# Where the last scaling of the output rows is done in an encoder step: VectorE alone, or VectorE and GpSimd

## What is computed

```python
def rmsnorm(x, g):
    xf = x.astype(jnp.float32)
    r = lax.rsqrt(jnp.mean(xf * xf, axis=-1, keepdims=True) + EPS)
    return (xf * r).astype(x.dtype) * g

def hier_moe(x, ...):
    ...                                  # top-1 group, top-2 experts of 16
    return x + out.reshape(bsz, L, D_MODEL)

y_prompt = rmsnorm(xp, norm_final)
y_sample = rmsnorm(xs, norm_final)
```

## Time and profile before

| | |
|---|---|
| median of three runs | 1203.53 us (1202.56 to 1205.54) |
| the profiled execution's own time | 1205.74 us |
| its span | 1204.0 us |
| TensorE busy, share of the span | 1144.2 us, 95% |
| VectorE busy | 715.8 us, 59% |
| ScalarE busy | 564.6 us, 47% |
| GpSimd busy | 120.6 us, 10% |
| mean granted TensorE clock | 0.983 of full speed |

### The profile page before, as it was taken

How to read it: one execution, slowest core, us unless ns; L and a number is a source line. 1 busy time by engine, 2 the same in 40 slices (tenths; PEclk the granted TensorE clock), 3 DMA queues, 4 the chain that set the end, 5 groups by cost and what they waited for, 6 DMA issues and landing times.

```text
span 1204.0 us, 18490 instructions
## 1 busy us (share of the span) xinstructions
PE 1144.2 (95%) x7908; PEld 1035.7 (86%) x7908; DVE 715.8 (59%) x850; ACT 564.6 (47%) x709; POOL 120.6 (10%) x147
## 2 busy tenths in 40 slices
PE   4999999999999999999899999999899999999994
PEld 4998779999987899999899999989757878788873
DVE  4424574775368743332434743534679998888884
ACT  4424473334386731221313632311166868778763
POOL 2002341000134100000000000000001000000051
PEclk9999998999999999999999999999899999999998
DMA  9231110222310222332435612201799999999995
GB/s 292 85 131 36 36 40 1 89 88 72 79 45 2 71 71 79 97 85 74 149 100 195 214 53 71 71 1 36 274 356 379 421 416 381 387 402 390 368 267 151
DMA packets 95038, 197.27 MB, mean 164 GB/s; under 512 B 4208, under 2 KB 71960, under 8 KB 82664
## 3 DMA queue, kind: packets, MB, share of 16 engines
q1 hardware_dynamic: 87328, 169.88, 40.2%
q0 software_dynamic: 5440, 18.76, 5.4%
q10 hardware_dynamic: 2184, 7.39, 1.5%
HBM read 178.41 MB, written 17.61 MB: 163 GB/s over the span
## 4 chain that ended last, share of the span: by engine, by line
PE 73%; DVE 10%; ACT 8%; issue 4%; DMA 4%; ACTq 0%; SPq 0%; POOL 0%; DVEq 0%; POOLq 0%
PE ps L2241 46%; PE ps L1032 6%; DVE buf_r L966 4%; ACT buf_r L959 3%; PE ps L1042 3%; PE ps L2646 2%; PE ps L2662 1%; DMA buf<-in_w_gate_e 1%; PE ps L2344 1%; PE ps L2373 1%; DMA buf<-in_w_in 1%; DVE buf_r L1181 1%; ACT buf_r L461 1%; PE ps L2374 1%; PE ps L2386 1%
## 5 line engine op out<-in xcount | busy, mean ns | idle before, releaser
L2241 PE MATMUL ps<-buf_r,buf_r 128*128 128x288 f32 (+1 forms) x4560 | 603.0, 293 | 12.8 <-DVE buf_r L465 6.5
L2241 PEld LDWEIGHTS ps<-buf_r,buf_r 128*128 128x128 f32 x4560 | 590.9, 190 | 17.3 <-issue 9.2
L966 DVE TENSOR_TENSOR buf_r<-buf,buf_r 128x2048 fp32r<-128x2048 f32 x92 | 205.1, 2284 | 0.0
L1032 PE MATMUL ps<-buf_r,buf_r 128*128 128x512 f32 x720 | 174.6, 398 | 0.0
L959 ACT CAST buf_r<-buf 128x2048 fp32r<-128x2048 f32 x92 | 170.9, 1908 | 0.1
L446 DVE TENSOR_TENSOR buf_r<-buf,buf_r 128x2048 fp32r<-128x2048 f32 (+2 forms) x49 | 107.5, 2196 | 103.8 <-ACT buf_r L440 103.7
L1032 PEld LDWEIGHTS ps<-buf_r,buf_r 128*128 128x128 f32 x720 | 133.4, 188 | 29.5 <-issue 0.5
L440 ACT CAST buf_r<-buf 128x2048 fp32r<-128x2048 f32 (+2 forms) x53 | 96.6, 1824 | 109.1 <-PE ps L2241 55.1
L1042 PE MATMUL ps<-buf_r,buf_r 128*128 128x512 f32 x384 | 89.8, 390 | 0.5 <-DVE buf_r L1209 0.5
L1042 PEld LDWEIGHTS ps<-buf_r,buf_r 128*128 128x128 f32 x384 | 72.0, 188 | 15.8 <-DVE buf_r L1209 0.9
L461 ACT CAST buf_r<-ps 128x512 fp32r<-128x512 f32 (+2 forms) x41 | 30.0, 731 | 75.9 <-PE ps L1016 63.2
(11 more groups left out here) (331 smaller groups left out, 1269.8 us busy)
## 6 DMA issues: line engine op xcount, KB each, us to landing
buf<-in_w_gate_e SPq DMA_DIRECT2D x32, 1024.0 KB, 8.3
buf<-in_w_up_e SPq DMA_DIRECT2D x32, 1024.0 KB, 7.9
buf<-in_w_down_e SPq DMA_DIRECT2D x32, 1024.0 KB, 7.4
buf<-in_w_in SPq DMA_DIRECT2D x16, 1024.0 KB, 5.5
buf<-in_w_in SPq DMA_DIRECT2D x17, 512.0 KB, 4.9
buf<-in_w_mem_kv SPq DMA_DIRECT2D x8, 1024.0 KB, 5.9
y_rows<-buf ACTq DMA_DIRECT2D x14, 512.0 KB, 8.0
buf<-in_x_prompt SPq DMA_DIRECT2D x8, 512.0 KB, 5.6
```

The source lines that it names most:

```text
L966: nc.vector.tensor_tensor(e_lo(t), e_raw(t), e_hi(t), ALU.subtract).then_inc(wl_ready, 1)
L1032: last = nc.tensor.matmul(bank(b), r32(a[:, k, :]), w[:, i, :], start=(k == 0 and j == 0), stop=(k == KD - 1 and j == 2))
L2241: last = nc.tensor.matmul(out, a, b, start=(k == 0 and j == 0), stop=(k == len(parts) - 1 and j == 2))
```

## The change

The order of the tail on VectorE becomes: add 0, add 1, finish 0, add 2, add 3, finish 2, add 4, finish 4. Chunks 1 and 3 are finished by GpSimd, each in two instructions: X times the row factor, a wait for the completion of that, then X times the gains. A new semaphore, fin_pool, counts these four. SyncE waits on it for chunks 1 and 3 and on fin_ready for the others, still in the order of the chunks.

```diff
@@ moe_sp
             for m, (t0, n) in enumerate(CH):
-                sp.wait_ge(fin_ready, m + 1)
+                if m % 2:
+                    sp.wait_ge(fin_pool, m + 1)
+                else:
+                    sp.wait_ge(fin_ready, m // 2 + 1)
                 dst = O["y_prompt"][0, t0:t0 + n, :] if m < 4 else O["y_sample"][0]
                 out_dma(sp, dst, X[:n, m, :], hn_stored)
@@ moe_pool
                 add_rows(pool, y_rows, R12O, 32)
+            pool.wait_ge(gains_loaded, 32)
+            for j, m in enumerate((1, 3)):
+                t0, n = CH[m]
+                pool.wait_ge(x3_ready, m + 1)
+                pool.wait_ge(ri_ready, N_F + m + 1)
+                pool.tensor_scalar(X[:n, m, :], X[:n, m, :], RI[:n, 17 + m:18 + m], None, ALU.mult).then_inc(fin_pool, 1)
+                pool.wait_ge(fin_pool, 2 * j + 1)
+                pool.tensor_tensor(X[:n, m, :], X[:n, m, :], NF[:n, :], ALU.mult).then_inc(fin_pool, 1)
@@ moe_dve
                 nc.vector.tensor_tensor(X[:n, m, :], X[:n, m, :], bank(SC_BANK[m], 2)[:n], ALU.add).then_inc(x3_ready, 1)
-                if m:
+                if m in (1, 3):
                     finish(m - 1)
             finish(NC_ - 1)
```

More of the change, by code:

```diff
@@ L521, in encoder_step @@
         fin_loaded = [sem(f"fin_loaded{i}") for i in range(2)]
-        sc_psum, x3_ready, fin_ready = (sem(n) for n in ("sc_psum", "x3_ready", "fin_ready"))
+        sc_psum, x3_ready, fin_ready, fin_pool = (sem(n) for n in ("sc_psum", "x3_ready", "fin_ready", "fin_pool"))
         yol_ready = sem("yol_ready")
```

## The result

| | before | after |
|---|---|---|
| median | 1203.53 us, 5 runs | 1209.36 us, 5 runs |
| lowest to highest | 1202.56 to 1205.54 | 1207.12 to 1211.62 |
| ratio of the runs | | 1.0043, 95% interval 1.0026 to 1.0059 |
| profiled execution | 1205.74 us, span 1204.0 | 1211.62 us, span 1209.9 |

What follows compares the result with a forecast made beforehand. VectorE bounds the tail for 7 us, then a latency chain; 0.45 us on the late last addition and 0.36 on the last finish give +0.81 us, so 1204.3 us from the 1203.53 median; range 1202.2 to 1207.2.

Steps and rivals of the forecast that it cites:

- What bounds the kernel: Tail: VectorE bound for 7 us, then a latency chain; removing two finishes gains 0.46 us, not 2.4.
- the price of the first step: GpSimd's multiplication of X by the row factor, chunks 1 and 3: taken as 1.05 us, lower bound 0.95.
- the upper bound: Most that GpSimd's multiplication by the row factor was taken to cost: 2.39 us, the two-input product's time.
- The rule of the Trainium skill: GpSimd runs one-input operations at roughly line rate; two-input ones take about twice as long as on VectorE, speaking against the change.
- The shut-out: VectorE's finishes and GpSimd's instructions exclude each other; a held finish ends 1.08 us behind GpSimd; additions from PSUM are free.
- the sum: Tail timeline with shut-out: last addition 0.45 us late, last finish 0.36 more, end +0.81 us; chance 0.65.
- d: Length of GpSimd's multiplication by the row factor, taken as 1.05 us; last finish ends at 1199.30 + 2d.
- The 0.12 us that a held instruction saves: GpSimd's instruction for chunk 3, held by finish 2, has 0.12 us of its start already behind it.
- Rival 1: Slow row-factor multiplication on GpSimd: +3.3 us at d = 2.3, +3.8 at 2.39 (1207.3); chance 0.08.
- its formula: Slow row-factor multiplication, finish 2 going first: last output issue at 1202.04 + d against 1200.62.
- The end of the span: Span ends 3.4 us after the last output DMA is issued.
- Rival 2: GpSimd's first multiplication starts late, its first d 5.0: +4.8 us, 1208.3; near +7 by the skill's figure; chance 0.03.

Runs made afterwards that it cites:

- a_second_alone: Kernel after without GpSimd's first step (row factor left out for chunks 1 and 3, time only): 1204.19 us, ratio 0.9996 to the kernel before.
- a_broadcast: Kernel after with GpSimd's first step written as a product with the row factor broadcast along the row: 1206.01 us, ratio 1.0013 to the kernel before.
- c_only3: Kernel after with only chunk 3 finished by GpSimd, chunk 1 back on VectorE: 1208.56 us, ratio 1.0030 to the kernel before.
- b_scalar: Kernel before plus four GpSimd multiplications by a row factor on scratch, beside VectorE's finishes: one execution, 1205.50 us.
- c_only1: Kernel after with only chunk 1 finished by GpSimd, chunk 3 by VectorE: 1205.12 us, ratio 1.0008 to the kernel before.

## Why the prediction was wrong

**What bounds the kernel**: right. The tail is a chain of latency behind a VectorE that is busy for 7 us, and taking two finishes out of it is worth 0.46 us; a_second_alone measured 0.45. That it came out so closely is in part luck: the same gain of addition 4 was 0.06 us in the first trace of the kernel after and 0.40 in the second, by when TensorE let addition 3 in.

**The step that failed is the price of the first step.** "I take 1.05, since it reads one tile as the cast does." It takes 2.83 to 2.86 us. I had put the upper bound at 2.39, as if a scalar could not cost more than a second tile. It does. The value lies above the upper bound, so the range was wrong from that line on. The numbers of the earlier trace rows are right, but they are those of casts and clearings; the trace of before has no row of GpSimd's arithmetic with a scalar, and I let the number of inputs stand for the form.

The prediction also said that "every one-input row is at 1 ns per column". That was not so. The groups of instructions of the kernel before have a selection, also with one input, beside a clearing of the same shape:

```profile
L1500 POOL TENSOR_SCALAR_AFFINE_SELECT buf<-buf 128x128 f32<-128x128 f32 x4 | 1.0, 282 | 0.1
...
L1494 POOL MEMSET buf<- 128x128 f32 x3 | 0.5, 204 | 0.0
```

The selection takes 282 ns for 128 columns, 2.2 ns per column, and the clearing 204. Read against the clearing of 1024 columns (952 ns), some 100 ns of it do not go with the width; taking the same for the selection, I estimate about 1.6 us for 1024 columns of it. It would not have given 2.85, but it says that one input has more than one price.

**The rule of the Trainium skill** that I weighed there (GPSIMD Engine Reference, Engine selection: one-input operations roughly at line rate) holds for the copy, 1.03 us, and not for this form, 2.77 to 2.86 us in four variants. Its advice to leave elementwise work to VectorE was right here.

**The shut-out**: the mechanism was right for the forms in the rows, and a_broadcast follows the sum to 0.14 us. The 0.12 us that a held instruction saves behind VectorE's end can't be read from the earlier trace rows, which shows no such selection alone; a_broadcast's held first step gives 0.15. For the scalar form the mechanism was wrong: VectorE was let in after 0.9 us. So "finish 2 is pushed by d, and the last second step by d again" did not happen; in the kernel after it is GpSimd's second step that loses 0.9 us to finish 2.

**Rival 1**, a slow first step, is what came true, and its course was right: finish 2 first, chunk 1's second step held, SyncE's chunk 4 behind chunk 3. With d = 2.85 its formula gives a last issue moved by 1.42 + 2.85 = +4.3 us; measured +3.3 and +3.6. It had the last finish take a turn between GpSimd's two instructions, which the scalar form made needless; without that turn the formula gives 0.9 us less, +3.4. I had given this rival 0.08, and priced it only up to 2.39.

**The end of the span**: I took the 3.4 us from last issue to end as fixed. It was 3.9. Chunk 4's DMA took 3.4 us to land where chunk 3's was issued right ahead of it (the kernel after, twice, and c_only3), against 2.9 in the kernel before; and GpSimd's own closing wait had become level with that landing. That is 0.5 us of the 3.8 to 4.1.

**Rival 2** (a late start of the first instruction of a kind): did not occur. The first scalar instruction began 0.22 to 0.23 us behind the row factor and took 2.86 us; the later ones took 2.83 and 2.84. The 0.1 us that I allowed for a hand-over was short there; between GpSimd's two steps (0.08 to 0.09) it fitted. The Trainium skill's 6 us for the first call of a freshly loaded kernel (GPSIMD Engine Reference, Instruction dispatch) was seen nowhere; whether this form needs such a load at all, no run shows.

**The size**: rival 1's course with d = 2.85, without the needless turn, and with the longer end gives +3.9 us, or 1207.4 on the median of before, already past the end of my range. The rest of the +5.8 is scatter ahead of the tail as far as the record shows, 1.8 us in the profiled pair; a second comparison gave 1.0031 [1.0016, 1.0045]. I had widened the range by 0.9 us for it on the low side and by nothing on the high side.

## What to carry to other kernels

Price an instruction on GpSimd by a row of the same form, and where there is none, measure it by itself on scratch in an idle stretch before moving work onto it: one tile with a scalar cost 2.8 us per 1024 columns, two tiles 2.34, one tile and a repeated column 1.90, a copy 1.03. Work taken off a busy engine gains only the latency it was holding up, here 0.46 us out of 2.4, while the chain that takes it over counts in full if its input comes last. The late chunk cost 3.0 us in the tail; the early one cost nothing up to the last issue, and 1.0 us behind it, because it held back the outputs. Before adding an engine, try the order on the one you have: that gave 0.5 to 0.6 us in the traces.

## What the runs showed that I had not expected

- GpSimd's scalar form is slower than its product of two tiles, 2.77 to 2.86 against 2.34 us, for a multiplication and an addition (2.80), with a row factor and with a constant alike.
- That form let VectorE's two-input instructions in from 0.9 us after its start on (finishes of 1.28 us when they asked 1.3, 2.1 and 2.7 us in, 1.48 at 0.70, 1.62 at 0.57), where the copy and the products kept them out to the end.
- GpSimd's closing wait ended 3.8 to 3.9 us behind its last instruction in all eleven kernels that end with arithmetic on GpSimd (10.4 to 11.1 us in the three where an indirect DMA is last, long before the end). So work of GpSimd that ends later than about 3.9 us before the last landing sets the end of the program: in b_scalar, whose scratch work nobody waited for, the last output was issued at 13.86 us and the span still ended at 20.68.
- Outputs issued in order behind one late chunk pile up: in c_only1 four of them held the DMA engines at full share, and the last landed 1.2 us later.
